# Latent stage of a two-block transformer kernel: inputs turned and split in the sum banks, up weights in two kept pieces

## Reference

```python
# shared keys and values of the latent attention
h = modulate(rmsnorm(x, norm_g), shift, scale)
c_kv, k_rope = jnp.split(h @ w_down, [KV_RANK], axis=-1)      # 1024 -> 256 + 32
c_kv = rmsnorm(c_kv, latent_g)
kv = (c_kv @ w_up).reshape(B, S, B_HEADS, NOPE_DIM + V_DIM)   # 256 -> 2048
# queries
h = modulate(rmsnorm(x, b_norm_g[j]), sh1, sc1)
cq = rmsnorm(h @ w_dq, q_g)                                   # 1024 -> 768
q = (cq @ w_uq).reshape(B, S, B_HEADS, NOPE_DIM + ROPE_DIM)   # 768 -> 1536
```

## Time and profile before

| | us |
|---|---|
| median of 3 runs | 2652.74 |
| range of the runs | 2651.41 to 2655.47 |
| the profiled execution, its own time | 2658.39 |
| its span in the trace | 2656.6 |
| the stage, from the first transpose (L1619) to the start of the latent attention | 642.2 to 731.8 |
| PE, DVE, ACT, POOL busy over the span | 2474.7, 1705.8, 1326.6, 91.9 |

### The profile page before, as it was taken

How to read it: one execution, slowest core, us unless ns; L and a number is a source line. 1 busy time by engine, 2 the same in 40 slices (tenths; PEclk the granted TensorE clock), 3 DMA queues, 4 the chain that set the end, 5 groups by cost and what they waited for, 6 DMA issues and landing times.

```text
span 2656.6 us, 31418 instructions
## 1 busy us (share of the span) xinstructions
PE 2474.7 (93%) x12658; PEld 2088.2 (79%) x12658; DVE 1705.8 (64%) x1536; ACT 1326.6 (50%) x1818; POOL 91.9 (3%) x121
## 2 busy tenths in 40 slices
PE   4988999998887999999999999899997999999999
PEld 3877777787777777778878888788886888987887
DVE  5757788787657777776544555645556555744555
ACT  3554777444554656643444444544445544444443
POOL 1000000100000000000000000100001000000000
PEclk8997999999998999999999999999999999999999
DMA  8713999984613978873644595335542455563553
GB/s 283 253 53 127 340 352 347 342 309 136 242 48 135 328 270 306 308 283 118 206 158 145 180 260 193 112 127 190 190 158 96 159 193 190 169 201 117 185 190 127
DMA packets 231296, 539.80 MB, mean 203 GB/s; under 512 B 21072, under 2 KB 29808, under 8 KB 231152
## 3 DMA queue, kind: packets, MB, share of 16 engines
q1 hardware_dynamic: 208992, 471.82, 51.0%
q0 software_dynamic: 15520, 59.77, 6.4%
q10 hardware_dynamic: 6640, 6.20, 1.2%
HBM read 533.54 MB, written 4.19 MB: 202 GB/s over the span
## 4 chain that ended last, share of the span: by engine, by line
PE 64%; DVE 15%; DMA 10%; ACT 6%; issue 3%; POOL 1%; SPq 1%; ACTq 0%; DVEq 0%
DVE w_low L2173 6%; PE pair L1008 6%; PE Y L1128 6%; PE Y L1130 6%; PE Y L1138 5%; PE pair L1051 4%; PE pair L1045 4%; PE pair L1046 4%; DMA raw<-in_exp_w_down 4%; DMA raw<-in_exp_w_gate 3%; PE pair L1016 3%; ACT w_high L1717 3%; PE pair L978 2%; PE pair L980 2%; PE pair L986 2%
## 5 line engine op out<-in xcount | busy, mean ns | idle before, releaser
L2173 DVE TENSOR_TENSOR w_low<-raw,w_high 128x2048 fp32r<-128x2048 f32 (+3 forms) x456 | 1021.4, 2246 | 583.7 <-ACT w_high L1717 581.6
L1717 ACT ACTIVATE w_high<-raw 128x1024 fp32r<-128x1024 f32 (+3 forms) x912 | 912.0, 1038 | 742.6 <-PE Y L1138 203.1
L1045 PE MATMUL pair<-w_high,hT 128*128 128x512 f32 (+1 forms) x612 | 240.7, 394 | 9.5 <-DVE hT L2229 5.2
L1046 PE MATMUL pair<-w_high,hT 128*128 128x512 f32 (+1 forms) x612 | 239.2, 391 | 0.0
L1128 PE MATMUL Y<-w_high,gated_high 128*128 128x512 f32 x528 | 205.8, 390 | 0.3 <-ACT w_high L1717 0.3
L1130 PE MATMUL Y<-w_high,gated_low 128*128 128x512 f32 x528 | 205.8, 390 | 0.0
L1008 PE MATMUL pair<-hT,w_high 128*128 128x512 f32 x768 | 183.0, 390 | 2.3 <-DVE work L2598 2.3
L1008 PEld LDWEIGHTS pair<-hT,w_high 128*128 128x128 f32 x768 | 142.5, 188 | 31.6 <-DVE work L2598 2.7
L1051 PE MATMUL pair<-w_low,hT 128*128 128x512 f32 (+1 forms) x612 | 152.5, 389 | 6.2 <-DVE w_low L2173 6.2
L1377 PE MATMUL pair<-w_high,rounded 128*128 128x512 f32 x384 | 154.8, 403 | 2.7 <-DVE gated_low L2498 2.7
L1378 PE MATMUL pair<-w_high,rounded 128*128 128x512 f32 x384 | 152.4, 397 | 0.0
(11 more groups left out here) (378 smaller groups left out, 4066.6 us busy)
## 6 DMA issues: line engine op xcount, KB each, us to landing
raw<-in_exp_w_gate SPq DMA_DIRECT2D x128, 512.0 KB, 4.5
raw<-in_exp_w_up SPq DMA_DIRECT2D x128, 512.0 KB, 4.8
raw<-in_exp_w_down SPq DMA_DIRECT2D x128, 512.0 KB, 4.6
raw<-in_w_up SPq DMA_DIRECT2D x128, 512.0 KB, 4.7
raw<-in_w_down SPq DMA_DIRECT2D x128, 512.0 KB, 4.3
work<-in_w_mod POOLq DMA_DIRECT2D x48, 1024.0 KB, 7.5
raw<-in_ret_w_in SPq DMA_DIRECT2D x96, 512.0 KB, 4.7
raw<-in_ret_w_out SPq DMA_DIRECT2D x32, 512.0 KB, 4.0
```

Of the source, the lines that this page charges most:

```text
L1045: nc.tensor.matmul(ps[:, b, 0:n], in_high[:, k0 + kk, bs], high[:, k, :], start=(kk == 0), stop=False)
L1046: nc.tensor.matmul(ps[:, b, 0:n], in_low[:, k0 + kk, bs], high[:, k, :], start=False, stop=False)
L1717: nc.scalar.activation(w_high[:, s % HIGH, part], raw[:, s % RAW, part], ACT.Copy).then_inc(high_ready, 1)
L2173: V.tensor_tensor(w_low[:, s % HIGH, 0:n], part, w_high[:, s % HIGH, 0:n].bitcast(F32), ALU.subtract).then_inc(low_ready, 1)
```

## The change

The transposes of `xn` go to the places `norm_ps`, in which blocks k and k + 4 share a bank, and one bank after another is reported to ACT. ACT reports each of its 16 evictions. DVE splits the key-value inputs two blocks at a time, the query inputs four at a time as before, and PE waits for the blocks of a product one by one.

The 768 query latents are turned into `Y` (`cq_ps`, two blocks to a bank) and reported by twos; ACT makes the high parts and DVE the low parts by twos, and `uq[0]` waits for them by twos (`cq_split`). Between the second and third product of `kv_up`, no `pair` tile is used.

The four chunks of `kv_up` (eight pieces of 128x512) become one chunk of two pieces of 128x2048. The four products use columns of the same two pieces, which are free only after the fourth.

DVE computes only the first half of modulation 20 ahead of the low part of `ckv`, the second half after it has scaled `cq`, and the first half of 21 after the low part of `cq`. POOL issues one load of 21 ahead of the inverse root for `cq` and one behind it.

```diff
@@ plan
-    p.kv_up = [p.proj("kv_up", j, size=512) for j in range(2)]
+    p.kv_piece = p.chunk("kv_up")
+    p.kv_up = p.fills(3) + [Use(p.take("use"), chunk=p.kv_piece)]
     p.cq_stat = p.stat(TB, Q_RANK)
-    p.cqT = p.fills(2)
-    p.cq_high = p.take("high", 2)
-    p.kv_up += [p.proj("kv_up", j, size=512) for j in range(2, 4)]
+    p.cq_high = p.take("high", 3)
@@ POOL
-            load_mods((21,))
+            load_mod(21, 0)
             inverse_rms(plan.cq_stat)
+            load_mod(21, 1)
@@ PE
-            for j in range(2):
-                for b in range(TB):
-                    pe.wait_ge(scaled, TB * lt.scaled + b + 1)
-                    for k in range(4 * j, 4 * j + 4):
-                        last = nc.tensor.transpose(Y[:, k * S + b * P:k * S + (b + 1) * P], xn[:, b, k * P:(k + 1) * P], ident)
+            pe.wait_ge(scaled, TB * lt.scaled + 1)
+            for bank in range(2):
+                turn_latent(0, bank)
+                turn_latent(0, bank + 4)
+            pe.wait_ge(scaled, TB * (lt.scaled + 1))
+            for bank in range(4):
+                for b in range(TB):
+                    if b or bank >= 2:
+                        turn_latent(b, bank)
+                        last = turn_latent(b, bank + 4)
                 last.then_inc(latent_turned, 1)
+            def kv_product(j):
+                use = plan.kv_up[j]
+                ps, ns = tokpair(pair(use)[:, :]), slice(512 * j, 512 * (j + 1))
+                wait_free(pe, use)
+                for k in range(2):
+                    s = 2 * plan.kv_piece + k
+                    high, low = w_high[:, s % HIGH, ns], w_low[:, s % HIGH, ns]
+                    wait_high(s, j // 2)
...
+                    wait_low(s)
...
+                    if j == 3:
+                        last.then_inc(piece_done, 1)
+                if j < 3:
+                    last.then_inc(fill_done, 1)
...
             pe.wait_ge(latent_ready, 2)
-            transposes(plan.cqT[0], cq, 0)
-            transposes(plan.cqT[1], cq, 4, 2)
-            token_product(plan.kv_up[2], 2)
-            token_product(plan.kv_up[3], 2)
-            for use in plan.cqT:
-                wait_emptied(pe, use)
+            for k in range(Q_RANK // P):
+                for b in range(TB):
+                    last = nc.tensor.transpose(cq_ps[k][:, b * P:(b + 1) * P], cq[:, b, k * P:(k + 1) * P], ident)
+                if k % 2:
+                    last.then_inc(cq_turned, 1)
+            kv_product(2)
+            kv_product(3)
-            token_product(plan.uq[0], 6, k0=2)
+            token_product(plan.uq[0], 6, k0=2, block_ready=cq_input)
@@ ACT
-                for j in range(2):
-                    se.wait_ge(latent_turned, j + 1)
...
+                for k in range(KD):
+                    se.wait_ge(latent_turned, k % 4 + 1)
...
                 if j == 1:
-                    high_of(hT_high[:, 2:6, :], plan.cqT[0], 4, cols[:, BQ_G:BQ_G + 4])
-                    high_of(hT_high[:, 6:8, :], plan.cqT[1], 2, cols[:, BQ_G + 4:BQ_G + 6])
+                    for k in range(Q_RANK // P):
+                        se.wait_ge(cq_turned, k // 2 + 1)
+                        last = nc.scalar.activation(hT_high[:, 2 + k, :], cq_ps[k], ACT.Identity, scale=cols[:, BQ_G + k:BQ_G + k + 1])
+                        if k % 2:
+                            last.then_inc(hT_high_made, 1)
@@ DVE
-            latent_inputs(0)
-            latent_inputs(1)
-            latent_inputs(2)
+            for k in range(0, KD, 2):
+                latent_inputs(0, k, 2)
+            latent_inputs(1, 0, 4)
             feed(2 * c + 3)
-            latent_inputs(3)
+            latent_inputs(1, 4, 4)
...
             feed(2 * plan.dq[1].chunk + 2)
-            mod_rows(20)
+            mod_half(20, 0)
             low_of(hT_low[:, 0:2, :], hT_high[:, 0:2, :], plan.ckvT, plan.ckv_high, 2, cols[:, LAT_G:LAT_G + 2])
-            feed(2 * plan.kv_up[0].chunk + 3)
-            mod_half(21, 0)
-            feed(2 * plan.kv_up[1].chunk + 2)
+            feed(2 * plan.kv_piece + 2)
             ve.wait_ge(rs_ready, plan.cq_stat + 1)
...
             last.then_inc(latent_ready, 1)
-            feed(2 * plan.kv_up[2].chunk + 2)
...
+            mod_half(20, 1)
+            feed(2 * plan.uq[0].chunk + 1)
+            for j in range(3):
+                ve.wait_ge(hT_high_made, plan.cq_high + j + 1)
+                for k in range(2 * j, 2 * j + 2):
+                    last = V.scalar_tensor_tensor(hT_low[:, 2 + k, :], cq_ps[k], cols[:, BQ_G + k:BQ_G + k + 1],
+                                                  hT_high[:, 2 + k, :].bitcast(F32), ALU.mult, ALU.subtract)
+                last.then_inc(cq_split, 1)
+            mod_half(21, 0)
             feed(2 * plan.uq[0].chunk + 1)
             mod_half(21, 1)
             feed(2 * plan.uq[0].chunk + 3)
```

More of the change, by code:

```diff
@@ L327, in make_plan @@
     lt.after = p.n["update"]
-    lt.stat, lt.scaled, lt.high = p.stat(TB, D), p.take("scaled"), p.take("high", 4)
+    lt.stat, lt.scaled, lt.high = p.stat(TB, D), p.take("scaled"), p.take("high", 2 * KD)
     p.kv_down = p.proj("kv_down", size=4 * (KV_RANK + ROPE))
@@ L546, in build @@
         norm_ps = [Y[:, 512 * (k % 4) + S * (k // 4):512 * (k % 4) + S * (k // 4 + 1)] for k in range(KD)]
+        cq_ps = [Y[:, S * k:S * (k + 1)] for k in range(Q_RANK // P)]
         pT_ps = Y[:, 0:1024].rearrange("p (h t) -> p h t", h=4)
@@ L808, in source @@
                 if kind == "kv_up":
-                    return w["kv_w_up"].rearrange("(k p) n -> p k n", p=P)[:, :, what[1] * 512:(what[1] + 1) * 512]
+                    return w["kv_w_up"].rearrange("(k p) n -> p k n", p=P)
                 if kind == "dq_tail":
@@ L1020, in wide_product, with token_product @@
                     last.then_inc(piece_done, 1)
-            def token_product(use, k_blocks=KD, n=512, other_half=None, inputs=(hT_high, hT_low), k0=0, ready=None, block_ready=None):
+            def token_product(use, k_blocks=KD, n=512, other_half=None, inputs=(hT_high, hT_low), k0=0, block_ready=None):
                 ps = tokpair(pair(use)[:, :])
@@ L1030, in token_product @@
                         wait_emptied(pe, other_half)
-                    if ready is not None:
-                        pe.wait_ge(latent_input, ready + j)
                     s = 2 * use.chunk + j
@@ L1620, in _, with kv_input, q_input, cq_input @@
                 last.then_inc(latent_turned, 1)
-            token_product(plan.kv_down, KD, KV_RANK + ROPE, inputs=for_kv, ready=1)
-            token_product(plan.dq[0], inputs=for_b, ready=3)
+            def kv_input(k):
+                pe.wait_ge(latent_input, k // 2 + 1)
+            def q_input(k):
+                pe.wait_ge(latent_input, KD // 2 + k // 4 + 1)
+            def cq_input(k):
+                pe.wait_ge(cq_split, k // 2 + 1)
+            def kv_product(j):
[7 more added lines that the diff above has]
+                    for b in range(TB):
+                        bs = slice(b * P, (b + 1) * P)
+                        nc.tensor.matmul(ps[:, b, :], hT_high[:, k, bs], high, start=(k == 0), stop=False)
+                        nc.tensor.matmul(ps[:, b, :], hT_low[:, k, bs], high, start=False, stop=False)
+                    wait_low(s)
+                    for b in range(TB):
+                        last = nc.tensor.matmul(ps[:, b, :], hT_high[:, k, b * P:(b + 1) * P], low, start=False, stop=(k == 1))
+                    if j == 3:
+                        last.then_inc(piece_done, 1)
+                if j < 3:
+                    last.then_inc(fill_done, 1)
@@ L1624, in _ @@
+            token_product(plan.kv_down, KD, KV_RANK + ROPE, inputs=for_kv, block_ready=kv_input)
+            token_product(plan.dq[0], inputs=for_b, block_ready=q_input)
             pe.wait_ge(latent_ready, 1)
@@ L1631, in _ @@
             last.then_inc(fill_done, 1)
-            token_product(plan.dq[1], KD, 256, inputs=for_b, ready=3)
+            token_product(plan.dq[1], KD, 256, inputs=for_b)
             wait_emptied(pe, plan.ckvT)
-            token_product(plan.kv_up[0], 2)
-            token_product(plan.kv_up[1], 2)
+            kv_product(0)
+            kv_product(1)
             pe.wait_ge(latent_ready, 2)
-            transposes(plan.cqT[0], cq, 0)
-            transposes(plan.cqT[1], cq, 4, 2)
-            token_product(plan.kv_up[2], 2)
-            token_product(plan.kv_up[3], 2)
-            for use in plan.cqT:
-                wait_emptied(pe, use)
+            pe.wait_ge(hT_high_made, lt.high + 2 * KD)
+            for k in range(Q_RANK // P):
+                for b in range(TB):
+                    last = nc.tensor.transpose(cq_ps[k][:, b * P:(b + 1) * P], cq[:, b, k * P:(k + 1) * P], ident)
[3 more added lines that the diff above has]
+            kv_product(3)
             def turn_keys(g):
```

25 lines of the change are left out of this document (10 added, 15 removed).

## The result

| | us | against before, 95% interval |
|---|---|---|
| before, as measured with it (4 runs) | 2652.07 | |
| changed (4 runs) | 2635.11 | 0.9934 [0.9914, 0.9954] |
| changed, measured once more (7 runs) | 2635.47 | 0.9942 [0.9920, 0.9965], before 2652.39 |
| changed, the profiled execution | 2630.56 | |

The account below looks back on a forecast made before the run. PE's waits and slow clock in the stage were taken as the bound. Gains of 2.3, 2.46, 5.16, 2.7 and 0 to 1.4 make 12.6 to 14.0; DVE's chain says 13.4, giving 2639.3 us, range 2634 to 2647 (8 in 10).

Parts of the forecast that it names:

- Latent inputs: Ahead of `kv_down`: PE starts at about 645.9 instead of 648.2, a gain of 2.3 us.
- The term put at nothing: Clock in `kv_down`: could add up to 1.5 us or rise later and take the 2.3; no change was counted.
- `dq`, nothing: From `dq[0]` to `kv_up`: nothing touched, so no gain; ACT's 2.0 us rounding ahead of `ckv`'s high part stays covered.
- `kv_up`, 2.46: PE's waits of 0.50, 1.49 and 0.47 us in `kv_up`, for parts and the scaled `cq`, go: 2.46 together.
- The tight second low part: In `kv_up`, the second piece's low part ends at 674.0 and PE needs it at 674.1: a tenth of slack.
- `cq`, 5.16 and up to 1.4 for the transposes: Before product 2 of `kv_up`: PE's 5.16 us idling goes; transposes of `cq` gain 0 to 1.4 at full clock.
- Clock of products 2 and 3: In `kv_up`, products 2 and 3 take 5.44 us instead of 8.17 with no gap ahead: 2.7 gained.
- DVE's chain as the bound: At `uq[0]`, the second piece's low part, behind modulation work, is ready at 692.1 instead of 705.5: gain 13.4 us.
- Modulation loads: Rival, 12 in 100: loads of halves 21, 22 and 23 come 1.6 us late each, 4.8 lost, gain 8.6, time 2644.
- The clock did not stay low: Rival, 7 in 100: PE stays at 1.2 GHz or the gap only shrinks; 7.9 us gained, time 2645.
- The stage's gain reached the whole: Rival, 8 in 100, claimed the opposite: the stage gains but the kernel doesn't, time 2650 to 2655.
- The held `w_high` slots: Rival, 3 in 100: slots held until product 3 delay `uq` loads, costing 31 us against 13.4; slower, 2670.

Follow-up runs that it names:

- low_first: The changed kernel with DVE making the low part of the second `uq[0]` piece ahead of the second half of modulation 21; stage 75.7 us, ratio 0.9953.
- ckv_in_sums: `low_first` with the key-value latents also turned into the free fourth sum bank; stage 73.7 us, ratio 0.9958 to the kernel before.

## Why the prediction was right

It gave 2639.3 and a range of 2634 to 2647; measured were 2635.1 and 2635.5, a little over 1 us from the range's lower end. The narrower range of the forecast itself, 2636.7 to 2641.7 (11 to 16 us gained), missed them: the medians give 17. The stage gained 15.4 and 14.3 in its two pairs of traces, where 13.4 was forecast. The mechanism held; its size was somewhat small.

*Latent inputs, 2.3 forecast: 2.08.* The split by twos costs 0.43 and 0.69 (forecast 0.4 and 0.65). The term put at nothing, that the clock rises sooner in `kv_down`, was mis-sized: `kv_down` took 1.21 less in the first trace and 0.66 less in the second against the second of before. The forecast said that PE, with 1.9 us for a pair of blocks on the low clock (that is half of the first piece less its low part, not the fourth it is called), doesn't starve. At full clock a pair takes 1.06, about as long as DVE's 1.05, and PE stopped once, for a quarter of a microsecond (642.69).

*`dq`, nothing: 0.00.* The ACT piece of 2.0 us ahead of the high part of `ckv` stayed covered; DVE stood 1.53 there and still had the first large low part made before PE asked.

*`kv_up`, 2.46: 3.12.* No wait for an eviction stood there; the other 0.66 is what the three stops cost beyond the idle time in the rows, some 0.2 each: the last matmul ahead of a stop no longer overlaps the next, and the first one behind it lasts longer (0.47 for 0.39). The tight second low part held in the first trace (it ended at 668.16, and PE asked at 668.41) and was 0.27 late in the second, where the large piece landed late. A wait of ACT for that piece was named as a sign of being wrong; there was one in both traces, 0.28 and 0.74. It cost nothing in the first and 0.4 in the second.

*`cq`, 5.16 and up to 1.4 for the transposes: 6.75.* The scaling ended at 671.04, ahead of the end of product 1 at 671.60, as forecast. The transposes took 1.23 and ran at full clock, in both traces.

*Clock of products 2 and 3, 2.7: 2.60.* Granted clock 1.00 instead of 0.66. The idle matmuls alone, in the kernel before, gave the same 2.6 in these products.

*DVE's chain as the bound, 13.4.* The late low part of `uq[0]` was forecast as the one that would stop PE, and it is the row with a wait (0.42), with none in the second trace. The chain was 1.5 shorter than written, since `kv_down` ended 1.2 sooner and all behind it moved. So the sum, 12.6 to 14.0, was too small by the clock of `kv_down` and the extra cost of the stops; the late low part of `uq[0]` took 0.4 back.

*Rivals.* Modulation loads were not late: DVE has no wait for one in either trace of the changed kernel. (The forecast's 687.2 and 688.8 for the landing are 0.3 more than 680.0 with 6.9 and 8.5, so its 1.6 should have been 1.3.) The margin was small: the runs that put the requests back, `low_first` and `ckv_in_sums`, have such waits. Landing was 5.6 to 8.6 us:

```profile
DMA to landing us min/median/max: 5.6/6.7/8.6
```

By the rule of the Trainium skill (DMA: Bandwidth & Descriptors, Anatomy of one DMA) a megabyte takes about 4.4 us, an estimate from its two figures. The trace again doesn't agree: its shortest is 5.6. The clock did not stay low. The stage's gain reached the whole: 15.4 and 14.3 in the traces, 17.0 and 16.9 by the medians. The held `w_high` slots cost nothing: the three `uq` pieces were rounded in one row of 4.59 us from 679.67, right behind the last eviction.

What stays open: single parts gained more in the stage than in the time (new latent inputs 5.3 and 6.8 against 1.6 and 4.8; idle matmuls 4.7 against 0.6; small pieces 7.8 against 2.5, or 4.0 by the ratio). The intervals are 2 to 4 us to each side, and a single trace catches one phase of the clock. No run tells whether something behind the stage gives a part back or adds to it, nor what the size of the `kv_up` pieces is worth apart from the place of the modulation halves.

## What to carry to other kernels

When one engine waits in a chain of short stages, look at what shares a buffer with the slow step: results that go to a bank nobody needs soon let the next product start before they are split. Slots counted in pieces prefetch in bytes what a piece holds, so small pieces in such a ring leave little time between a load's request and its use, and whatever delays a request then shows. Fill work on an in-order engine (here the modulation halves) belongs behind the value that another engine waits for, but each move of it also moves the requests that hang on it.
